# Second layer's projections with weights moving instead of activations, and the head pairs moved along

## The reference

```python
p = rmsnorm(x, attn_norm[1]) @ odd_w_in          # 2048 x 2888
qc, cl, qi, ki, wi = split(p)                    # 2048, 256, 8 x 64, 64, 8 columns
cl = rmsnorm(cl, c_kv_norm)                      # the latent
score = sum_h relu(qi_h @ ki.T) * wi_h           # index score, 8 heads
sel = top_k(score, 64)                           # within the causal chunk
q_lat = qc_h @ w_uk_h.T                          # 16 heads
s = q_lat @ cl[sel].T / sqrt(128) + bias
oc_h = softmax(s) @ cl[sel] @ w_uv_h
x = x + concat(oc) @ odd_w_out
```

## Time and profile before

| | us |
|---|---|
| median of 3 runs (lowest, highest) | 2467.67 (2466.76, 2467.9) |
| profiled execution: span, first to last instruction | 2465.2 |
| what the median run has around such a span | 2.5 |
| layer 1's index products | 1109.8 to 1154.3 |
| keys and values | to 1179.0 |
| queries and attention | to 1290.6 |

### The profile page before, as it was taken

One profiled execution on the slowest core, in us unless ns is written; L12 is line 12 of the kernel. 1 busy time (PEld: TensorE's weight loads), 2 busy tenths in 40 slices (PEclk: granted clock), 3 DMA queues, 4 the chain that ended last, 5 costly groups with the idle time before them and its releaser, 6 DMA issues.

```text
span 2465.2 us, 32147 instructions
## 1 busy us (share of the span) xinstructions
PE 2458.4 (100%) x11360; PEld 2039.8 (83%) x11360; DVE 1723.4 (70%) x2633; ACT 1206.7 (49%) x1593; POOL 59.7 (2%) x81
## 2 busy tenths in 40 slices
PE   9999999999999999999999999999999999999999
PEld 8888888888888888888888888888888888888777
DVE  7766786666666665667867666666666566789886
ACT  6454555444444444445554544444444444555774
POOL 1000000000000000000220000000000000100000
PEclk9999999999999999999999999999999999999999
DMA  7555556666666655557545665666665555755454
GB/s 245 183 176 179 176 173 196 195 194 191 194 193 191 194 194 191 195 169 216 165 143 174 194 195 188 196 195 192 192 193 195 192 195 193 223 185 166 150 185 157
DMA packets 284588, 463.17 MB, mean 188 GB/s; under 512 B 18237, under 2 KB 101135, under 8 KB 283976
## 3 DMA queue, kind: packets, MB, share of 16 engines
q1 hardware_dynamic: 282224, 453.64, 57.5%
q0 software_dynamic: 1984, 8.14, 1.0%
q10 hardware_dynamic: 280, 0.08, 0.0%
HBM read 459.65 MB, written 2.14 MB: 187 GB/s over the span
## 4 chain that ended last, share of the span: by engine, by line
PE 95%; DVE 3%; ACT 1%; issue 1%; POOL 0%; DVEq 0%; ACTq 0%; POOLq 0%
PE PG L262 85%; PE PG L238 3%; PE PG L237 1%; DVE ws L214 1%; DVE cacc L1557 1%; PE PO L902 1%; PE PS L845 1%; PE PS L888 0%; PE PG L250 0%; PE PG L271 0%; ACT ws L208 0%; PE PG L1334 0%; PE PS L846 0%; PE PO L903 0%; DVE pT L1227 0%
## 5 line engine op out<-in xcount | busy, mean ns | idle before, releaser
L214 DVE TENSOR_TENSOR ws<-raw,ws 128x1024 fp32r<-128x1024 f32 x859 | 1053.3, 1228 | 668.6 <-ACT ws L208 661.8
L262 PE MATMUL PG<-ws,hs 128*128 128x512 f32 x6336 | 1455.3, 390 | 0.1
L208 ACT ACTIVATE ws<-raw 128x1024 fp32r<-128x1024 f32 x859 | 908.8, 1059 | 1063.6 <-PE PG L262 989.1
L262 PEld LDWEIGHTS PG<-ws,hs 128*128 128x128 f32 x6336 | 1184.8, 188 | 245.8 <-issue 0.3
L262 PE MATMUL PG<-ws,fs 128*128 128x512 f32 x2112 | 479.0, 389 | 0.0
L262 PEld LDWEIGHTS PG<-ws,fs 128*128 128x128 f32 x2112 | 396.4, 188 | 82.3
L262 PE MATMUL PG<-ws,os 128*128 128x512 f32 x1104 | 253.7, 390 | 0.2 <-DVE ws L214 0.2
L262 PEld LDWEIGHTS PG<-ws,os 128*128 128x128 f32 x1104 | 206.5, 188 | 43.2 <-DVE ws L214 0.6
L608 DVE STREAM_TRANSPOSE turnb<-qst 32x256 f32<-32x256 f32 x352 | 153.3, 436 | 7.2
L238 PE MATMUL PG<-hs,ws 128*128 128x512 f32 x368 | 128.9, 393 | 0.0
L1557 DVE SCALAR_TENSOR_TENSOR cacc<-hc,convw,cacc 128x256 f32<-128x256 f32 x232 | 100.1, 488 | 0.0
(11 more groups left out here) (322 smaller groups left out, 922.3 us busy)
## 6 DMA issues: line engine op xcount, KB each, us to landing
raw<-in_w_gate SPq DMA_DIRECT2D x176, 512.0 KB, 3.5
raw<-in_w_up SPq DMA_DIRECT2D x176, 512.0 KB, 3.5
raw<-in_w_down SPq DMA_DIRECT2D x176, 512.0 KB, 3.6
raw<-in_even_w_in SPq DMA_DIRECT2D x128, 256.0 KB, 3.0
raw<-in_w_in SPq DMA_DIRECT2D x52, 512.0 KB, 3.4
raw<-in_odd_w_in SPq DMA_DIRECT2D x44, 512.0 KB, 3.5
raw<-in_even_w_in SPq DMA_DIRECT2D x32, 512.0 KB, 3.8
raw<-in_even_w_out SPq DMA_DIRECT2D x32, 512.0 KB, 4.7
```

Of the source, the lines that this page charges most:

```text
L208: e.activation(ws[j % RING][:, :, 0, :], raw[:, j % RING], ACT.Copy).then_inc(s_hi, 1)
L214: e.tensor_tensor(w[:, :, 1, :], raw[:, j % RING], w[:, :, 0, :].bitcast(F32), ALU.subtract).then_inc(s_lo, 1)
L262: ins = e.matmul(out[:, b, :], x_, w[:, kk, :, h, :], start=first and kk == 0 and n == 0, stop=last and kk == 1 and n == 2)
```

## The change

- gI becomes a narrow group (eight units of 328 columns: 256 of index queries, 64 of keys, 8 index weights) and a wide one (the latent and the other 256 index query columns), both with weights moving.
- Query group 0 (four heads) is computed before the keys and values, the other three in gQ, all by `mul_W`. The index scores move from gI and gU into it, the top search from gU and gQ into gU.
- Index queries and queries are drained scaled by ScalarE (`wide_out`, `queries_out`) and turned by VectorE in 16 blocks of 32 each (`turn_rows`); keys and latent are turned by TensorE.
- The latent's norm is taken from sums along the free axis.
- kC and vC are drained by ScalarE alone; the values are read where they lie, without GpSimd's copy.
- The division moves to ScalarE (`c_norm`). Pair j's scores follow unit 4 + 4j, its flips three units later, its mix five units later, so pairs 5 to 7 lie in the output product.
- The output product takes five units each of groups 0 and 1, then the last three of both in turn, then groups 2 and 3. Its group 1 rows are turned by TensorE after unit 21.

The diff, cut to its core:

```diff
-    gI = Seg(1, [4] * 4, [0, 2, 0, 2])
-    gU = Seg(2, [1] * 4, [0, 0, 2, 0])
-    gQ = Seg(4, [4, 4], [0, 2])
+    gI = Seg(1, [8, 8], [0, 2])
+    gQ0 = Seg(1, [8], [0])
+    gU = Seg(2, [1] * 4, [2, 0, 0, 0])
+    gQ = Seg(1, [8] * 3, [2, 0, 2])
...
+    def mul_narrow(e, bank, jj, j, first, last):
+        w_ = narrow_ws(jj)
+        for kk in (0, 1):
+            for b in (0, 1):
+                xh, xl = (hs[:, 2 * j + kk, h, b * P:(b + 1) * P] for h in (0, 1))
+                for n, (x_, h) in enumerate(((xh, 0), (xh, 1), (xl, 0))):
+                    ins = e.matmul(PG[:, bank + b, 0:NARROW], x_, w_[:, kk, h, :], start=first and kk == 0 and n == 0, stop=last and kk == 1 and n == 2)
+        return ins
...
+    def turn_rows(e, dst, part):
+        for n in part:
+            r, c = 32 * (n // 4), 32 * (n % 4)
+            blocks_in = nat_q[r:r + 32].rearrange("p b (t c) -> p b t c", c=P)[:, :, :, c:c + 32]
+            blocks_out = dst[c:c + 32].rearrange("p t (b s) -> p b t s", s=P)[:, :, :, r:r + 32]
+            ins = e.transpose(blocks_out, blocks_in)
+        return ins
...
+    def keys_turn(e):
+        e.wait_ge(s_drain, gI.group(0, 0) + 3)
...
+    def latent_turn(e):
+        e.wait_ge(s_drain, gI.group(0, 1) + 3)
...
     def score(e, h):
-        w(e, "kic", 2)
-        e.wait_ge(s_drain, gI.group(0, 2 + h // 4) + 3)
+        w(e, "iT", 1)
+        w(e, "kic", 1)
...
-            w(e, "dup", 2)
-            e.matmul(PO[:, 0, 0:S], dup[0:64, :], kst[0:64, 0, :], start=True, stop=True)
+        group_pe(e, gI, 0, 0, mul_narrow, {1: lambda: rows_turn(e, "n2", 3, gD0)}, lambda j: w(e, "n2lo", 2 * j + 2))
+        group_pe(e, gI, 0, 1, W_mul(hs), {1: lambda: keys_turn(e)})
...
+        def wide_out(_):
+            q = gI.banks[1]
+            e.wait_ge(s_mm, gI.end(0, 1) + RING)
+            for b in (0, 1):
+                e.activation(q_even[:, b, :], PG[:, q + b, 0:256], ACT.Square, scale=rnT[:, b:b + 1], accum_out=c_sums[:, b:b + 1]).then_inc(sem("csq"), 1)
+            for b in (0, 1):
+                ins = e.activation(nat_q[:, b, 0:256], PG[:, q + b, 256:512], ACT.Copy, scale=rnT[:, b:b + 1])
+            ins.then_inc(sem("in"), 1)
+        def split(e, u, j):
+            (hi_narrow if j < RING else hi)(e, u, j)
+        group_side(e, gI, 0, 0, split, narrow_out, {0: lambda: norm_act(e, "n2"), 1: lambda: rows_hi(e, "n2", 3, 1)})
+        group_side(e, gI, 0, 1, hi, wide_out, {1: lambda: keys_out(e)})
...
+    def queries_out(e, g, seg, k):
+        e.wait_ge(s_mm, seg.end(0, k) + RING)
+        w(e, "qc", 1)
+        w(e, "qT" if g else "iT", g or 1)
+        for b in (0, 1):
+            ins = e.activation(nat_q[:, b, :], PG[:, seg.banks[k] + b, :], ACT.Copy, scale=q_column[:, b:b + 1])
+        ins.then_inc(s_drain, 1)
...
+    def q_turn(e, g, n):
+        if n == 0:
+            e.wait_ge(s_drain, (gQ.group(0, g - 1) if g else gQ0.group(0, 0)) + 3)
+            w(e, "CS", 2 * g - 2)
+        ins = turn_rows(e, q_buffer(g), quarter_of(n))
+        if n == 3:
+            ins.then_inc(sem("qT"), 1)
...
+    def q0_pe(e):
+        group_pe(e, gQ0, 0, 0, W_mul(hs), {2: lambda: latent_turn(e), 3: lambda: score(e, 0), 4: lambda: score(e, 2), 5: lambda: score(e, 4), 6: lambda: score(e, 6)})
+    def q0_act(e):
+        def relus(h):
+            relu(e, h)
+            relu(e, h + 1)
+        group_side(e, gQ0, 0, 0, hi, lambda _: queries_out(e, 0, gQ0, 0),
+                   {0: lambda: latent_log(e), 1: lambda: latent_out(e), 2: lambda: latent_hi(e), 3: lambda: relus(0), 4: lambda: relus(2), 5: lambda: relus(4), 6: lambda: relus(6)})
...
+            add(e, h + 1)
+        hk = {("early", n): (lambda n=n: i_turn(e, n)) for n in (1, 2, 3)}
+        hk["early", 0] = lambda: (latent_mean(e), i_turn(e, 0))
+        hk.update({0: lambda: latent_root(e), 2: lambda: latent_lo(e), 3: lambda: adds(0), 4: lambda: adds(2), 5: lambda: adds(4), 6: lambda: adds(6)})
+        group_side(e, gQ0, 0, 0, lo, lambda _: None, hk)
+    phase(sp=stream(gQ0, lambda i, k, j: wide_cols(Wo, j, 0), wide=1), pe=q0_pe, act=q0_act, dve=q0_dve)
...
                     if k % 2 == 0:
-                        e.activation(kC[:, bass.ds(8 * i + 4 * (k // 2), 2), :], key_pair(gU.banks[k]), ACT.Copy).then_inc(s_cross, 1)
+                        t = 8 * i + 4 * (k // 2)
+                        q = gU.banks[k]
+                        e.activation(kC[:, t:t + 4, :].rearrange("p (a h) s -> p a (h s)", a=2), PG[:, q:q + 2, :], ACT.Copy).then_inc(s_drain, 1)
...
+                        e.activation(vC[:, :, c:c + 512], PO[:, :, :], ACT.Copy).then_inc(s_drain, 1)
+                group_side(e, gU, i, k, hi, drain)
         body(0)
         body(1)
...
+                group_side(e, gU, i, k, lo, lambda _: None, {0: lambda: top(e, 4 * i + k)})
...
+    def c_norm(e, j):
+        w(e, "Cr", j + 1)
+        for h in (0, 1):
+            for c, src in enumerate((slice(0, S), slice(S, 384))):
+                n = 2 * h + c
+                e.activation(ts[:, h, src], ts[:, h, src], ACT.Copy, scale=rs[:, n:n + 1]).then_inc(sem("Cn"), 1)
+    def c_V(e, j):
...
+    def c_steps(name, e):
+        at = {}
+        def put(x, f, early=False):
+            x = ("early", x) if early else x
+            at[x] = (lambda f0=at[x]: (f0(), f())) if x in at else f
+        if name == "dve":
+            put(0, lambda: selection(e))
+            for g in range(4):
+                for n in range(4):
+                    put(8 * g + n - (g > 0), lambda g=g, n=n: q_turn(e, g, n), early=True)
+        for j in range(8):
+            b, last = 4 + 4 * j, j == 7
+            if name == "pe":
+                put(b, lambda j=j: c_S(e, j))
+                put(b + 3, lambda j=j: flips(e, "C", j))
+                put(b + 5 - last, lambda j=j: c_V(e, j))
+            elif name == "act":
+                put(b + 1, lambda j=j: exps(e, "C", j))
+                put(b + 2, lambda j=j: c_norm(e, j))
+                put(b + 3, lambda j=j: flipped(e, "C", j))
+                put(b + 6 - last, lambda j=j: out_hi(e, "C", j, 2 * j), early=last)
+            else:
+                put(b + 1, lambda j=j: c_max(e, j), early=True)
+                put(b + 2, lambda j=j: c_reciprocal(e, j), early=True)
+                put(b + 6 - last, lambda j=j: out_lo(e, "C", j, 2 * j), early=last)
...
+    oo_order = [(g, n) for g in (0, 1) for n in range(5)] + [(g, n) for n in (5, 6, 7) for g in (0, 1)] + [(g, n) for g in (2, 3) for n in range(8)]
+    oo_ends = {14: 0, 15: 1, 23: 2, 31: 3}
...
+    def oo_pe(e):
+        hk = steps_of("pe", e, 24, 32)
+        hk[21] = lambda: (w(e, "CpT", 8), rows_turn(e, "n3", 1, gOO))
+        for x, (g, n) in enumerate(oo_order):
...
+        hk = steps_of("act", e, 24, 32)
+        hk.update({19: lambda: rows_hi(e, "n3", 0, 3), 22: lambda: rows_hi(e, "n3", 1, 3), 28: lambda: rows_hi(e, "n3", 2, 3)})
...
+    def oo_dve(e):
+        hk = steps_of("dve", e, 24, 32)
+        hk.update({x: (lambda x=x: rows_blocks(e, "n3", 0, quarter_of(x - 15))) for x in range(15, 19)})
+        hk.update({x: (lambda x=x: rows_blocks(e, "n3", 2, quarter_of(x - 24))) for x in range(24, 28)})
+        hk.update({20: lambda: rows_lo(e, "n3", 0, 3), 23: lambda: rows_lo(e, "n3", 1, 3), 29: lambda: rows_lo(e, "n3", 2, 3)})
...
```

More of the change, by code:

```diff
@@ L226, in load @@
         e.dma_start(dst, src).then_inc(s_raw[j % RING], 16)
[L228 to L241, removed]
     def mul_N(e, bank, j, k0, lhs, first, last):
@@ L717, in norm_second, with residual, narrows, split_hi @@
         w(e, p + "D", 6)
[L719 to L733, removed]
     def hooked(e, fns):
         return {j: (lambda f=f: f(e)) for j, f in fns.items()}
-    def residual(seg, W, lhs, p, gain, unit_wait, pe_hooks={}, act_hooks={}, dve_hooks={}, free=None):
+    def residual(seg, W, lhs, p, gain, unit_wait, pe_hooks={}, act_hooks={}, dve_hooks={}, free=None, narrow_next=False):
         each = 4 if seg.groups[0] == 8 else 2
+        def narrows(u):
+            return narrow_next and u >= seg.ub + seg.U
+        def split_hi(e, u, j):
+            (hi_narrow if narrows(u) else hi)(e, u, j)
+        def split_lo(e, u, j):
+            (lo_narrow if narrows(u) else lo)(e, u, j)
         def pe(e):
@@ L1309, in cst_pe, with idx_sp @@
-    def cst_pe(e):
-        w(e, "csq", 1)
-        w(e, "kic", 2)
-        e.matmul(PO[:, 0, 0:S], ones[:], sq[:, 0, :], start=True, stop=False)
-        e.matmul(PO[:, 0, 0:S], ones[:], sq[:, 1, :], start=False, stop=True).then_inc(sem("cms"), 1)
-    phase(sp=idx_load, pe=idx_pe, act=idx_act, dve=idx_dve)
+    def idx_sp(e):
+        for j in range(8):
+            e.wait_ge(s_lo, gI.unit(0, j) + 1)
+            src = Wo.rearrange("(t p) n -> p t n", p=P)[:, 2 * j:2 * j + 2, 2560:2560 + NARROW]
+            e.dma_start(narrow_raw(j), src).then_inc(s_raw[j % RING], 16)
+        for j in range(8):
+            load(e, gI, 0, 8 + j, wide_cols(Wo, j, 2048), 1)
@@ L1344, in values, with body @@
```

(23 more changed lines are left out.)

339 lines of the change are left out of this document (171 added, 168 removed).

## The result

The changed kernel takes 2486.25 us (median of 4 runs, 2485.99 to 2488.38) against 2467.45 for the kernel before: 1.0079 times as long, interval 1.0066 to 1.0091. It is slower, as forecast, but by 18.8 us where 11.0 were predicted, and 0.25 us above the range.

A forecast was written before the change was run, and what follows sets the result against it. TensorE, always busy at full clock, was taken as the bound, so every new wait adds in full: -5.7 us of work plus new waits gave +11.0, span 2476.2, median 2478.7 us, range 2466 to 2486.

The forecast's parts named there:

- Products and other work: TensorE's matmuls, transposes, removed bursts and old waits: products gain 4.8, other work 0.4, old waits 0.5; 5.7 us gained.
- The waits: New TensorE waits at index scores, first attention scores, pair flips and third norm: 5.6 + 2.3 + 0.1 + 1.6 + 4.5 + 2.6 us.
- Wait A: Latent's transposes and index scores: TensorE waits for the latent and VectorE's 16 turned index query blocks, 5.6 us.
- Wait B: First pair's attention scores: TensorE waits for VectorE's 16 blocks of query group 0, 2.3 us.
- Wait D: Output product: turning group 1's third-norm rows waits for group 0's low halves from VectorE, 2.6 us.
- Wait C: Flips of each pair wait for softmax division on ScalarE: 0.1, four times 0.4, three times 1.5; 6.2 us.
- The sum: All work gains and new waits in TensorE's span added up: +11.0 us, span 2465.2 to 2476.2.
- No wait counts: Rival: VectorE's blocks are ready in time, so only the 5.7 us gain remains, 2462.0 us; chance 0.12.
- Single waits only: Rival: index-score, first-attention-score and third-norm waits come, the flips' few tenths vanish; +4.8, 2472.5 us; chance 0.22.
- The bias table: Rival: its 11.2 us GpSimd transfer holds up the wide weight loads; 2483 us, 2485 with GpSimd's disturbance; chance 0.14.

The follow-up runs named there:

- version without waits: Changed kernel: index scores and third norm's rows later, maxima first, division on VectorE, eight query blocks earlier, pair 4's output halves first in their step; 2461.37 us, ratio 0.9977.
- three waits mended: Changed kernel with index scores later, maxima first, division back on VectorE and third norm's group 1 rows turned later; 2466.85 us, ratio 0.9998.
- first blocks earlier: Changed kernel with eight of query group 0's sixteen blocks turned in the key and value product steps; 2483.86 us, ratio 1.007.

## Why the prediction was right in sign and wrong in size

- **Products and other work, -5.7**: right. The version without waits gains 5.7 us in the median and 5.5 between the two ends of the changed stretch. A product of 328 columns takes 3.57 / 24 = 0.149 us (1110.00 to 1113.57, where the next burst starts), 0.147 taken.
- **The waits, 16.7 together**: the working counts from start to start, so the listed idle times are to be taken with the 0.16 that each gap is longer: 17.6 + 1.8 = 19.4.
- **Wait A, 5.6**: 0.63 + 4.42 = 5.05 listed, 5.4 as gaps. The blocks' cycle of 3.05 us from the earlier trace rows held; the pieces in between were a little shorter than their sum.
- **Wait B, 2.3**: 2.41 listed, 2.6 as a gap. **Wait D, 2.6**: 2.65 and 2.8. Both right within 0.3.
- **Wait C, 6.2**: 7.5 listed, 8.6 as gaps, and the term that was sized most wrongly. The 0.4 for pairs 2, 4, 6 and 7 measured 0.36 (0.5 as gaps). For pairs 1, 3 and 5, taken at 1.5, they were 1.9 to 2.2 (2.0 to 2.4). The working put the division behind ScalarE's own queue and forgot its other input: the reciprocal, behind a block and a low half on VectorE. That half meets the bias sums of GpSimd. I had priced this meeting at wait B only, from the earlier trace rows; it came here, at 1.1 us (2.33 against 1.23), while at B, priced at up to 1.6, the longest low half took 1.38. By the Trainium skill (SBUF — State Buffer, Who interferes with whom) only the port pair shared by VectorE and GpSimd contends, as an exclusive lock, and of VectorE's instructions one with a single input in SBUF stays clear of it while one with two does not; the block beside the bias sums, 1.78 with or without them, and the low half, 2.33 against 1.23, agree.
- **The sum, +11.0, is the step that failed.** It added each wait at its own length and took TensorE's work to run at full clock whatever it had waited for. The clock of 1.00 was read from a kernel that never waits, and carried over to one that does. The low clock behind the waits cost 5.7 us in the profiled execution; keeping TensorE busy through the same waits gives 5.5 back, so this is shown and not only read off. Beside it the waits were 19.4 as gaps, not 16.7, of which C is 2.4, and the work was 0.3 lighter by the spans: 11.0 + 5.7 + 2.7 - 0.3 = 19.1 for the 19.0 measured. The slow work is twice what the mis-sized waits make.
- **Rivals.** "No wait counts" (2462.0) is not this kernel, but it is what becomes of it with the waits mended: 2461.37. "Single waits only" fell with the 7.5 us of C. The bias table did not hold up the loads: no wait on a weight unit is in the view of 1090 to 1410. No rival held what happened, a cost beside the waits that grows with them.

The order of the fixes tells the same: no single one of them brought the kernel within 10 us of the kernel before, since each left waits at the other places, with the low clock behind some of them.

## What to carry to other kernels

Where TensorE is the bound and never waits, a wait such as those here (1.9 to 4.4 us) costs its length and then, perhaps, slow work behind it; price both, from bursts of the same shape before and behind. Mend waits together before judging a change, since one mended alone can be given back in clock behind another. When single executions are compared by their spans, look at the last products too: here the clock there made up to 1.8 us. For each operation that a wait ends on, list all its inputs and the queue in front of each, the small ones (a reciprocal of four numbers) too.

## What the hardware did that I had not expected

The granted clock fell to 0.50 in the middle of a kernel in which TensorE is 99% busy. Which waits it follows is not fixed by their length: in the changed kernel's profiled execution a wait of 2.24 us left it at 1.00 and one of 2.41 did not; in the kernel with the rows turned later the flips' wait of 2.22 had 0.50 behind it; with three waits mended, one of 2.4 had none. With the first blocks earlier, one of 1.9 had it (flips of pair 5) and one of 2.6 did not (D). Even executions of one kernel differ, 2479.06 us at a mean clock of 0.998 and 2482.08 to 2482.96 at 0.996. What picks the waits is open. The Trainium skill (TensorE: Matmul & The Clock Gate, Part 1) says "the default state is throttled, and activity releases the throttle"; that idle transposes alone keep the clock at 1.00 through the same waits agrees with it.
